# Other orders at the layer norms, the first input and the last chunk of a two-block fp32 kernel

## What is computed

```python
u = x * (1.0 + sc1) + sh1
y = mixer(u)            # layer 0: gated linear attention, layer 1: chunk attention
x = layer_norm(ALPHA * x + (1.0 + g1) * y, ln_g[i, 0], ln_b[i, 0])
u = x * (1.0 + sc2) + sh2
y = square(relu(u @ w1)) @ w2
x = layer_norm(ALPHA * x + (1.0 + g2) * y, ln_g[i, 1], ln_b[i, 1])
```

## Time and profile before

| | |
|---|---|
| median of 3 runs | 1099.0 us (1097.58 to 1099.05) |
| profiled execution, its own time | 1096.28 us |
| its span in the profile | 1094.6 us |
| TensorE busy, share of the span | 1042.9 us, 95% |
| VectorE busy | 804.7 us, 74% |
| ScalarE busy | 506.4 us, 46% |
| GpSimd busy | 67.8 us, 6% |
| mean granted TensorE clock | 0.974 of full |

### The profile page before, as it was taken

The page is one execution under the profiler, slowest core; times in us unless marked ns, Lnnn a source line. Parts: engine busy times, 40 slices in busy tenths (PEclk is TensorE's granted clock), DMA queues, the critical chain, the costliest instruction groups (busy, mean ns, idle before and its releaser), DMA issues. The chain is left out here.

```text
span 1094.6 us, 16545 instructions
## 1 busy us (share of the span) xinstructions
PE 1042.9 (95%) x6776; PEld 934.5 (85%) x6776; DVE 804.7 (74%) x1105; ACT 506.4 (46%) x681; POOL 67.8 (6%) x143
## 2 busy tenths in 40 slices
PE   7999989999999999999999998999899989999995
PEld 7987779898898898879898997788798879999995
DVE  3498888989887867568776557668774858777775
ACT  2474434343432766534433334533346455555553
POOL 2001210000000121000000000100000000000000
PEclk9999998999999899999999999899899999999998
DMA  9969766899886474325955453543333435555551
GB/s 342 378 230 325 270 231 246 304 339 339 322 319 226 157 257 145 120 112 180 378 186 193 165 193 131 176 146 125 116 116 116 162 123 173 182 198 184 176 190 59
DMA packets 35051, 227.94 MB, mean 208 GB/s; under 512 B 4096, under 2 KB 4224, under 8 KB 10144
## 3 DMA queue, kind: packets, MB, share of 16 engines
q1 hardware_dynamic: 25232, 167.01, 43.4%
q0 software_dynamic: 9744, 59.87, 14.6%
HBM read 225.82 MB, written 1.05 MB: 207 GB/s over the span
## 5 line engine op out<-in xcount | busy, mean ns | idle before, releaser
L1445 DVE TENSOR_TENSOR weight_lo<-weight_raw,weight_hi 128x2048 fp32r<-128x2048 f32 (+1 forms) x188 | 361.6, 1926 | 106.1 <-ACT weight_hi L1027 105.8
L421 PE MATMUL ps<-act_hi,weight_hi 128*128 128x256 f32 x1336 | 337.0, 290 | 2.7 <-DVE act_lo L1570 2.7
L1027 ACT ACTIVATE weight_hi<-weight_raw 128x2048 fp32r<-128x2048 f32 (+2 forms) x168 | 299.4, 1786 | 78.9 <-PE ps L421 76.7
L421 PE MATMUL ps<-act_lo,weight_hi 128*128 128x256 f32 x1336 | 332.4, 286 | 0.0
L421 PEld LDWEIGHTS ps<-act_hi,weight_hi 128*128 128x128 f32 x1336 | 259.8, 194 | 12.8 <-issue 10.5
L421 PEld LDWEIGHTS ps<-act_lo,weight_hi 128*128 128x128 f32 x1336 | 260.3, 195 | 3.2 <-issue 1.0
L421 PE MATMUL ps<-act_hi,weight_lo 128*128 128x256 f32 x1336 | 182.4, 283 | 0.0
L421 PEld LDWEIGHTS ps<-act_hi,weight_lo 128*128 128x128 f32 x1336 | 169.2, 191 | 0.4
L421 PE MATMUL ps<-weight_hi,mlp_hi 128*128 128x512 f32 x256 | 101.8, 398 | 0.0
L421 PE MATMUL ps<-weight_hi,mlp_lo 128*128 128x512 f32 x256 | 100.9, 394 | 0.0
L1209 ACT ACTIVATE mlp_hi<-mlp_relu 128x512 fp32r<-128x512 f32 x32 | 20.3, 633 | 156.1 <-DVE mlp_relu L1870 148.8
(11 more groups left out here) (319 smaller groups left out, 1345.9 us busy)
## 6 DMA issues: line engine op xcount, KB each, us to landing
weight_raw<-weights SPq DMA_DIRECT2D x144, 1024.0 KB, 5.0
ada_raw<-ada POOLq DMA_DIRECT2D x48, 1024.0 KB, 6.5
weight_raw<-weights SPq DMA_DIRECT2D x23, 512.0 KB, 3.6
row_g<-ln_rows POOLq DMA_DIRECT2D x4, 512.0 KB, 4.3
row_b<-ln_rows POOLq DMA_DIRECT2D x4, 512.0 KB, 6.6
att_bias<-rel_bias POOLq DMA_DIRECT2D x16, 128.0 KB, 3.1
square<-ada_rows POOLq DMA_DIRECT2D x3, 512.0 KB, 3.9
dev<-x_in SPq DMA_DIRECT2D x1, 1024.0 KB, 5.7
```

The costliest lines, as they stand in the source:

```text
L421: return e.matmul(o, a, b, start=start, stop=False, skip_group_check=True)
L1027: e.activation(weight_hi[h][:, 0:size], weight_raw[r][:, 0:size], ACT.Copy).then_inc(hi_full[h], 1)
L1445: ins = e.tensor_tensor(weight_lo[h][:, c], weight_raw[r][:, c], weight_hi[h][:, c].bitcast(F32), ALU.subtract)
```

## The change

It reorders steps and moves no data that was not moved before. (1) First input: VectorE splits chunks 0, 1, 2 after tiles 2, 5, 7 and TensorE begins them at 2, 6, 7. (2) Norm 0: the split of chunk 17 comes in quarters: one between `ln_first` and `ln_second`, two after that, one between the halves of `input_lo`. (3) `ln_shift` of the first token half, and at norm 3 `square_root`, stand between the add and `bn_stats` of the third part. (4) `input_lo_half` alternates residues of tiles 0 to 3 with full values of 4 to 7. (5) Last chunk: ScalarE splits it after it has filled `conv_cv`; VectorE splits it by halves, one before it waits for the sigmoid and one before it waits for the high part; `last_tail` moves 3 products ahead of TensorE's wait. (6) Final norm: one column half of each token half is first multiplied by the weights on VectorE (`by_final_row`), and then by the root on ScalarE; the stores follow the new order.

```diff
@@ sync_program
-            for h in range(4):
-                e.wait_ge(final_in, h + 1)
-                c = slice(h % 2 * HALF, (h % 2 + 1) * HALF)
-                e.dma_start(out[:, h // 2, c], res[:, h // 2, c]).then_inc(stored, 16)
+            for t, n, made in ((0, 1, final_in), (0, 0, final_scaled), (1, 0, final_in), (1, 1, final_scaled)):
+                e.wait_ge(made, t + 1)
+                c = slice(n * HALF, (n + 1) * HALF)
+                e.dma_start(out[:, t, c], res[:, t, c]).then_inc(stored, 16)
@@ tensor_program
+            def last_tail(inputs):
+                (one, a_hi, a_lo), (two, b_hi, b_lo) = inputs
+                j1, j2 = TAILS[5]
+                e.wait_ge(*one)
+                row_half(j1, 5, 0, a_hi, a_lo, 0, 1, False)
+                for lo in (False, True):
+                    rows_of(j1, 5, 1, 0, a_hi, a_lo, 0, 1, False, lo)
+                e.wait_ge(*two)
...
+                rows_of(j1, 5, 1, 1, a_hi, a_lo, 0, 1, False, False)
+                rows_of(j1, 5, 1, 1, a_hi, a_lo, 0, 1, False, True).then_inc(chunk_done, 1)
+                for n in range(2):
+                    rows_of(j2, 5, 1, n, b_hi, b_lo, 0, 1, False, False)
+                    rows_of(j2, 5, 1, n, b_hi, b_lo, 0, 1, False, True).then_inc(chunk_done if n else y_bank, 1)
...
-            first = ((0, work_tiles(W["gk"], 1), P, 3), (1, work_tiles(W["q0"]), 256, 5),
+            first = ((0, work_tiles(W["gk"], 1), P, 2), (1, work_tiles(W["q0"]), 256, 6),
                      (2, [(q1_ps[:, n, :], 4) for n in range(2)], 256, 7))
@@ scalar_program
-            split_hi(down_chunk(2, FT2 - 1))
-            conv(FT2 - 1)
+            conv(FT2 - 1, down_chunk(2, FT2 - 1))
             for t in range(ST):
                 for n in range(2):
                     row_squares(5, t, n)
+            for t in range(ST):
+                c = slice(t * HALF, (t + 1) * HALF)
+                e.wait_ge(final_row_scaled, t + 1)
+                e.wait_ge(row_pow, ROOT_AT[5] + t + 1)
+                e.activation(res[:, t, c], dev_rows[:, t, c], ACT.Copy, scale=row_root[:, t, 3:4]).then_inc(final_scaled, 1)
@@ first_input
-                    if f in (2, 4, 6):
-                        split_lo(f // 2 - 1)
+                    if f in (2, 5, 7):
+                        split_lo((2, 5, 7).index(f))
@@ input_lo_half
-                e.wait_ge(x_turned, 4 * at + 2 * t + 2)
-                for k in range(4, KT):
...
-                    full_value(at, k, full[:, k, :], turned_tile(at, t, k))
-                for k in range(KT):
...
+                for k in range(4):
+                    residue(k)
+                    if k == 0:
+                        e.wait_ge(x_turned, 4 * at + 2 * t + 2)
+                    if t:
+                        e.wait_ge(hi_in, HI_AT[at] + k + 9)
+                        e.wait_ge(lo_in, LO_AT[at] + k + 5)
+                    full_value(at, k + 4, full[:, k + 4, :], turned_tile(at, t, k + 4))
+                for k in range(4, KT):
+                    residue(k)
@@ ln_part(at, t, n, between=None)
                 i = own.of(e.tensor_tensor(z, z, res[:, t, n * HALF:(n + 1) * HALF], ALU.add))
+                if between:
+                    between()
                 e.wait_ge(dve_step, i)
@@ ln_first
-                step = ln_part(at, 1, 0)
-                ln_shift(at, 0)
+                step = ln_part(at, 1, 0, lambda: ln_shift(at, 0))
@@ vector_program, norm 0
-            split_lo(J_OUT0 + 4)
             ln_first(0)
+            split_lo(J_OUT0 + 4, 0, 4)
             ln_second(0)
-            input_lo(0)
+            split_lo(J_OUT0 + 4, 1, 4)
+            split_lo(J_OUT0 + 4, 2, 4)
+            input_lo(0, lambda: split_lo(J_OUT0 + 4, 3, 4))
@@ vector_program, norm 3
-            step = ln_part(3, 1, 0)
-            square_root(3, 0)
+            step = ln_part(3, 1, 0, lambda: square_root(3, 0))
@@ vector_program, conv
+                if wait_lo is not None:
+                    split_lo(wait_lo, 0, 2)
                 e.wait_ge(conv_sig, i + 1)
...
+                if wait_lo is not None:
+                    split_lo(wait_lo, 1, 2)
                 e.wait_ge(hid_hi_in, 32 + i + 1)
...
-            split_lo(down_chunk(2, FT2 - 1))
-            conv(FT2 - 1)
+            conv(FT2 - 1, wait_lo=down_chunk(2, FT2 - 1))
+            def by_final_row(t):
+                c = slice(t * HALF, (t + 1) * HALF)
+                e.wait_ge(x_added, 4 * 2 + 3 * t + 1)
+                e.tensor_tensor(dev_rows[:, t, c], res[:, t, c], gate_rows[:, c], ALU.mult).then_inc(final_row_scaled, 1)
             def last_half(t):
+                c = slice((1 - t) * HALF, (2 - t) * HALF)
                 e.wait_ge(row_pow, ROOT_AT[5] + t + 1)
-                for n in range(2):
...
             for n in range(2):
                 add_part(5, 0, n)
+            e.wait_ge(final_row_in, 16)
+            by_final_row(0)
             add_part(5, 1, 0)
             square_root(5, 0)
             add_part(5, 1, 1)
-            e.wait_ge(final_row_in, 16)
             last_half(0)
             square_root(5, 1)
+            by_final_row(1)
             last_half(1)
```

More of the change, by code:

```diff
@@ L360, in build @@
                              "mix_lo_in", "o_hi_in"))
+        final_row_scaled, final_scaled = sem("final_row_scaled"), sem("final_scaled")
         sigmoid_in, pool_gated, att_gated, merge_sum, merge_cast, merged, final_in = (
@@ L524, in tail @@
                     rows_of(j2, at, 1, n, b_hi, b_lo, b0, nk, False, True).then_inc(chunk_done if n else y_bank, 1)
+            def last_tail(inputs):
[6 more added lines that the diff above has]
+                e.wait_ge(*two)
+                e.wait_ge(hi_full[j2 % N_SPLIT], j2 // N_SPLIT + 1)
+                for n in range(2):
+                    rows_of(j2, 5, 0, n, b_hi, b_lo, 0, 1, False, False)
+                    if n == 0:
+                        e.wait_ge(lo_full[j2 % N_SPLIT], j2 // N_SPLIT + 1)
+                    rows_of(j2, 5, 0, n, b_hi, b_lo, 0, 1, False, True).then_inc(y_bank, 1)
+                rows_of(j1, 5, 1, 1, a_hi, a_lo, 0, 1, False, False)
+                rows_of(j1, 5, 1, 1, a_hi, a_lo, 0, 1, False, True).then_inc(chunk_done, 1)
+                for n in range(2):
+                    rows_of(j2, 5, 1, n, b_hi, b_lo, 0, 1, False, False)
+                    rows_of(j2, 5, 1, n, b_hi, b_lo, 0, 1, False, True).then_inc(chunk_done if n else y_bank, 1)
             def turn(at, t):
@@ L782, in up_down @@
                     mods_of("m3", 3, 0, 16)
-                tail(at + 1, [((hid_lo_in, h0 + i + 1), hid_hi[m][i % 2], hid_lo[m][i % 2], 0)
-                              for i in (n_blocks - 2, n_blocks - 1)], tiles)
+                if m == 2:
+                    last_tail([((hid_lo_in, h0 + i + 1), hid_hi[m][i % 2], hid_lo[m][i % 2])
+                               for i in (n_blocks - 2, n_blocks - 1)])
+                else:
+                    tail(at + 1, [((hid_lo_in, h0 + i + 1), hid_hi[m][i % 2], hid_lo[m][i % 2], 0)
+                                  for i in (n_blocks - 2, n_blocks - 1)], tiles)
             up_down(0, 0)
@@ L1560, in full_value, with input_lo @@
                 ins.then_inc(full_in, 1)
-            def input_lo(at):
+            def input_lo(at, between=None):
                 def residue(k):
@@ L1575, in input_lo @@
                 for a in (0, 4):
+                    if a and between:
+                        between()
                     e.wait_ge(x_turned, 4 * at + 3 + a // 4)
@@ L1586, in input_lo_half, with residue @@
                     e.wait_ge(scale_in, at + 1)
-                e.wait_ge(x_turned, 4 * at + 2 * t + 2)
-                for k in range(4, KT):
-                    if t:
-                        e.wait_ge(hi_in, HI_AT[at] + k + 5)
-                        e.wait_ge(lo_in, LO_AT[at] + k + 1)
-                    full_value(at, k, full[:, k, :], turned_tile(at, t, k))
-                for k in range(KT):
+                def residue(k):
                     e.wait_ge(hi_in, HI_AT[at] + 12 * t + (2 * k + 2 if k < 4 else k + 5))
@@ L1612, in vector_program, with ln_part @@
             GATES = ("ra", "rb", "rc", "rd")
-            def ln_part(at, t, n):
+            def ln_part(at, t, n, between=None):
                 z = dev_rows[:, t, n * HALF:(n + 1) * HALF]
@@ L2180, in vector_program, with conv @@
             split_lo(HELD[4])
-            def conv(i, half_lo=None, whole_lo=None):
+            def conv(i, half_lo=None, whole_lo=None, wait_lo=None):
                 w, p = W[f"cv{i}"], i % 2
```

5 lines of the change are left out of this document (2 added, 3 removed).

## The result

The changed kernel takes 1087.8 us (median of 4 runs, 1086.0 to 1089.95); the kernel before took 1098.3 beside it. The ratio is 0.9906, 95% interval 0.9885 to 0.9927, so 10.5 us off by medians, where 6.5 were forecast; the range ended at 1088.0, 0.2 above the result. Measured again in two later sessions, the ratio is 0.9930 (0.9908 to 0.9953) and 0.9917 (0.9893 to 0.9940), 7.9 and 8.9 us by medians. Over the four later sessions the kernel before has a median of 1094.0 in 88 runs (1089.6 to 1098.7). The changed one has 1086.4 in 16 runs (1082.3 to 1089.95), the four of the first session among them: 7.7 us. The first session's four runs of the kernel before, 1097.2 to 1099.05, are not among the 88, of which only 12 reach 1097.2; why both kernels stood higher in that session is not shown. The profiled execution took 1087.7.

What follows compares the result with a forecast made beforehand. TensorE, busy 1042.9 of 1094.6 us, bounds the kernel; gains come from its idle time or half clock. Terms 1.0 + 1.1 + 1.3 + 0 + 1.3 + 1.8 = 6.5 off the median 1099.0 give 1092.5, range 1088 to 1096.5.

Steps and rivals of the forecast that it cites:

- First input: Start of the kernel: splitting one tile later removes TensorE's 1.20 us wait for VectorE; 1.0 us gained, bounds 0 and 1.3.
- near 39: Sign of a right forecast in the first input: the last of its eight loads lands near 39 us.
- Norm 0: Moving chunk 17's split saves 1.5 us, less 0.4 for a stretched power: 1.1, bounds 0 and 1.5.
- Norm 1: Alternating residues with full values brings the first residue 1.3 us earlier at half clock; lower bound 0.8.
- rival (a): Clock does not fall at norm 1: 1.0 us more; likewise in first input, gain 8 to 9, 1090.5; chance 0.17.
- Norm 2: Only the first half's turn comes 0.6 us earlier; the second half's chain ends last, so 0.
- Norm 3: Earlier root brings the second turn 0.8 us forward, a residue before full values another 0.5: 1.3 in all.
- Last chunk and end: Reordered splits and products give 1.4 us at the last product, final norm and stores 0.4: 1.8, bounds 1.0 and 2.2.
- what a place gives should stay: Attention and merge stages are untouched and TensorE hardly waits for weights there, so each place's gain should last.
- rival (b): Gains hide at first input and norm 0, half clock lasts longer at two norms: 3.0 us, 1096; chance 0.12.
- (c): Whole kernel: no change within 0.2% (2.2 us), steps work but every lower bound holds, 1097; chance 0.07.
- (d): Weight stream: chunk 20 lands late and TensorE waits for it, kernel slower, above 1101.2; chance 0.02.

Runs made afterwards that it cites:

- the kernel before with dummies: Kernel before, with TensorE given short dummy 128x128 products (results unused) while it waits for turned rows at norms 0 to 4: 1087.1 us, ratio 0.9943.
- the other four parts: First input, alternation, norm 0, and last chunk with final norm, each put alone into the kernel before: ratios 0.9983, 0.9969, 0.9966, 0.9973.
- dummies in a long form: Changed kernel with the longest groups of dummy 128x128 products in TensorE's waits at norms 0 to 4 and before the second attention: 1088.5 us, ratio 0.9948.

## Why the prediction was right, and where it failed

**First input** (1.0, bounds 0 and 1.3): 0 or below in the first pair of profiles, where the load was issued 0.4 earlier and landed at 41.0 after 40.5, and not near 39; over all profiles about 2 by medians, above the upper bound. That the load's landing decides was read from one execution, in which TensorE took it up within 0.1 us. It is so in the first pair alone, and in most others TensorE gets to the landed load late, in the old order later than in the new one.

**Norm 0** (1.1): the pause is 1.37 and 1.12 shorter. VectorE took up its last part at 158.43, 0.04 after TensorE's last product instead of 1.54; that, the power of 0.93 for "about 1.0" and the quarters without a wait of TensorE came as written. Of it 0.7 went into a longer half clock (5.87 for 4.14) in the first profile, none in the later ones.

**Norm 1** (1.3): 1.28 in the pause, and with the clock up TensorE waits 0.83 for the second half, as rival (a) had it. The clock did not fall in the first profile, and the stage is 2.5 us shorter. In the second and third it fell for 3.4 us inside that stage, and the stage was as short all the same (29.1 us), as the 0.83 wait then went: here the clock had slack. The pause's 1.28 is no gain of its own, though. In the old order the stage takes 31.5 to 31.7 us with 6.8 us of half clock, 30.2 to 30.4 with 3.4, and 29.2 with none (the kernel before with dummies, whose pause is as long as before, 4.25). In the new order it takes 29.0 to 29.3 in all ten profiles, with 3.4 us of half clock in two of them and none in the others. At full clock the 1.28 end in the wait for the second half's rows. Rival (a) gave 1.0 more than the forecast from a turn at 362.3; by its own rows it is 364.12 - 362.3 - 1.3 = 0.5. The turn came at 361.56, and the stage is 1.2 better than the pause.

**Norm 2** (0): 0. **Norm 3** (1.3): 1.44; the second turn is 0.76 nearer to norm 3's last product (0.8 forecast), by the root, as found alone (0.72), the rest by the residue ahead of the full values, with nothing left of the 0.58 wait. That rest isn't seen alone, as the clock fell over the second turn in the alternation's own profile. By the Trainium skill (SBUF — State Buffer, section Who interferes with whom) the power beside `bn_stats` would not be stretched and those beside a split or `by_final_row(1)` would; the runs agree with 0.54, 0.93 and 0.93.

**Last chunk and end** (1.8): 1.4 to 1.5 at the last product. Behind it 0.4 was expected and 0.03 measured: the issue came 0.23 earlier (4.38 for 4.61), and the second of two stores back to back landed 2.73 after its issue, where it had been 2.44. Mis-sized is the term for what follows the last product: root and stores together gave 0.03 for 0.4.

**What failed** is the sentence that attention and merge are left alone and so "what a place gives should stay". The sum took each pause's shortening as it stands, 6.5 in all, and the clock of all the rest as fixed. Two things were found in its place. At equal clock the steps bring 5.0 and not 6.5. Norm 1 keeps only 0.2 of its 1.28 when the clock is up; with that, what the profiles show at the six places still adds up to some 6, and the rest of the gap is not explained. And the clock of the rest moved: 3.2 us come from a mean clock of 0.982 instead of 0.978 (an estimate by the line above), which lies mostly in the second attention (92.0 to 93.3 us for 96.4 in the profiles) and in the stage behind norm 1, where half clock costs up to 2.5 us in the old order and next to nothing in the new one. That 5.0 and 3.2 together come near the forecast's 6.5 is luck. Rival (a) had the mechanism, but only at norm 1 and the first input, at a chance of 0.17.

The other part is the level: 6.5 were taken off a median of three runs, 1099.0, and 88 later runs of the same kernel have 1094.0. The profiled execution of 1096.3 stood beside it with a clock of 0.974; the spread that this clock implies was not put into the range, which covered the bounds of the steps alone. Of rival (b) the first input's 0 and the longer half clock after norm 0 came in the first profile, its time did not; (c) and (d) did not come about, and chunk 20 was never waited for.

**Open** is why the clock falls where it does. With nothing in the stage changed, the half clock lasts 6.8 us at norm 1 in the kernel before and 3.4 in the one with the new first input alone; in the second attention it lasts 10.2 in both profiles of the kernel before and in that of the earlier shift and root, 6.8 or less in those of the other four parts. That the changed kernel avoids the longest stretches there is measured. By which of its steps is open: alternation and norm 0 each alone have no run below a clock of 0.979, but one profile of each part and none of the kernel before above 0.974 are too few to tell an edit's work from chance.

## What to carry to other kernels

Where the granted clock differs between runs of one kernel, take its time against that clock over many runs before a few microseconds are forecast, and put that spread into the range. Shifting waits by a microsecond can move the stretches at half clock in stages that the edit doesn't touch, and this share doesn't add over edits, while the steps' own share did within the scatter. A pause that gets shorter is worth less where full clock would only lengthen the next wait: look there for what that wait depends on before the pause is counted. Filling waits ahead of a restart with dummy products is worth more than most reorderings here (6.5 us for the kernel before, 1081.8 to 1082.7 us in all for the changed one, the fastest version), if the dummies end before the rows are there and wait for no bank. Where another engine sets the next wait, as at norm 3, they give little or move the half clock behind that wait.

## What was unexpected of the hardware

One program's mean granted clock ranges from 0.974 to 0.984, and its time by 9 us, of which 7 go with the clock (0.70 us for each 0.001). Full clock alone doesn't bring its price back: with dummies in a long form the clock was 0.994 and the time 1088.5, above that of the changed kernel at 0.982. A store of twice the size issued once ended the span no earlier than two back to back (9.61 and 9.62 us behind the last product).
